# Attention outputs made feature-major, and projection panels moved between attention units and into the delta rule's scan

## What is computed

```python
# layer 0 of block one; H=8 heads of 64, causal (one block of 256 keys)
a_out = moba_attention(split_heads(q, MOBA_HEADS, MOBA_HEAD_DIM),
                       split_heads(k, MOBA_HEADS, MOBA_HEAD_DIM),
                       split_heads(v, MOBA_HEADS, MOBA_HEAD_DIM))
b_out = multiscale_pool(p, pool_w[i], pool_scale[i])
mix = jnp.concatenate([a_out, b_out], axis=-1) @ ev_w_out[i]
# both layers of block one; 4 heads of 256, keys and values from mem_n
q = (xn @ wq).reshape(B, S, XATTN_HEADS, XATTN_HEAD_DIM)
k, v = jnp.split(mem_n @ wkv, 2, axis=-1)
p = jax.nn.softmax(s, axis=-1).astype(v.dtype)
o = jnp.einsum('bhsm,bmhd->bshd', p, v).reshape(B, S, D)
return o @ wo
# layer 1 of block one: scan over 4 chunks of 64 tokens, per head
def step(state, inp):
    v_new = u_n - jnp.einsum('bhck,bhkv->bhcv', w_n, state)
    o = (jnp.einsum('bhck,bhkv->bhcv', qd_n, state)
         + jnp.einsum('bhij,bhjv->bhiv', qk_n, v_new))
    state = state * gl_n[..., None, None] + jnp.einsum('bhck,bhcv->bhkv', kd_n, v_new)
    return state, o
# both layers of block two: four attentions of 4 heads of 64; the first is
p = p[:, 0] - lam * p[:, 1]
o = sweep_query_blocks(block, q)
o = rmsnorm_2(o, norm_g) * (1.0 - lam_init)
y = jnp.concatenate([o_a, o_b, o_c, o_d], axis=-1) @ w_out[l]
```

## Time and profile before

| | us |
|---|---|
| runs | 2847.32, 2847.70, 2850.68 |
| median | 2847.7 |
| profiled execution | 2859.73 |
| its span, first to last instruction | 2857.9 |
| PE busy | 2739.3 (96%) |
| DVE busy | 1721.6 (60%) |
| ACT busy | 1309.5 (46%) |

### The profile page before, as it was taken

One profiled execution on the slowest core, in us unless ns is written; L12 is line 12 of the kernel. 1 busy time (PEld: TensorE's weight loads), 2 busy tenths in 40 slices (PEclk: granted clock), 3 DMA queues, 4 the chain that ended last, 5 costly groups with the idle time before them and its releaser, 6 DMA issues.

```text
span 2857.9 us, 39543 instructions
## 1 busy us (share of the span) xinstructions
PE 2739.3 (96%) x13974; PEld 2286.0 (80%) x13974; DVE 1721.6 (60%) x2575; ACT 1309.5 (46%) x1909; POOL 27.1 (1%) x40
## 2 busy tenths in 40 slices
PE   8999999997999999998999999899999999999998
PEld 7686898885778988885998886687878878787876
...
PEclk9899999896999999999999999899999999999999
...
GB/s 315 68 158 109 200 176 175 95 96 21 155 110 184 183 178 178 144 151 159 195 176 171 130 134 104 185 378 329 377 323 346 359 321 381 329 372 320 358 352 284
DMA packets 87635, 627.38 MB, mean 220 GB/s; under 512 B 9760, under 2 KB 9920, under 8 KB 12672
## 3 DMA queue, kind: packets, MB, share of 16 engines
...
...
## 4 chain that ended last, share of the span: by engine, by line
PE 94%; DVE 3%; ACT 1%; issue 1%; DMA 0%; DVEq 0%; SPq 0%; ACTq 0%
PE bank L775 21%; PE bank L668 14%; PE bank L523 11%; PE bank L803 11%; PE bank L682 6%; PE bank L618 6%; PE bank L534 6%; PE bank L864 6%; PE bank L590 2%; PE bank L566 2%; PE bank L913 1%; PE bank L818 1%; PE bank L745 1%; PE bank L579 1%; PE bank L790 1%
## 5 line engine op out<-in xcount | busy, mean ns | idle before, releaser
L1257 ACT ACTIVATE sb_parts<-sb_ring 128x1024 fp32r<-128x1024 f32 x873 | 873.0, 1052 | 95.6 <-PE bank L682 47.3
L1866 DVE TENSOR_TENSOR sb_parts<-sb_ring,sb_parts 128x1024 fp32r<-128x1024 f32 x675 | 787.0, 1219 | 6.3 <-ACT sb_parts L1257 6.3
L775 PE MATMUL bank<-sb_parts 128*128 128x512 f32 x2688 | 662.0, 396 | 8.2 <-DVE sb_parts L1866 5.7
L775 PEld LDWEIGHTS bank<-sb_parts 128*128 128x128 f32 x2688 | 495.6, 188 | 118.0 <-issue 9.5
L668 PE MATMUL bank<-sb_parts 128*128 128x256 f32 x3168 | 391.5, 286 | 20.1 <-DVE sb_parts L1830 20.1
L668 PEld LDWEIGHTS bank<-sb_parts 128*128 128x128 f32 x3168 | 390.3, 195 | 22.9 <-issue 20.8
L803 PE MATMUL bank<-sb_parts 128*128 128x512 f32 x1344 | 323.8, 390 | 0.0
L803 PEld LDWEIGHTS bank<-sb_parts 128*128 128x128 f32 x1344 | 251.7, 188 | 52.1
L1257 ACT ACTIVATE sb_REG<-bank 128x512 f32<-128x512 f32 (+3 forms) x118 | 67.8, 575 | 444.5 <-PE bank L523 224.3
L523 PE MATMUL bank<-sb_XT,sb_ring 128*128 128x256 f32 x1152 | 259.5, 387 | 6.9 <-DVE sb_XT L1698 3.9
L523 PEld LDWEIGHTS bank<-sb_XT,sb_ring 128*128 128x128 f32 x1152 | 222.7, 194 | 41.3 <-issue 10.4
...
## 6 DMA issues: line engine op xcount, KB each, us to landing
...
```

The costliest lines, as they stand in the source:

```text
L775: m = nc.tensor.matmul(banks[par][:, :], x[:, k, :], w[:, cols], start=k == 0 and t == 0, stop=k == KD - 1 and t == 2, skip_group_check=True)
L1257: return nc.scalar.activation(out, in_, ACT.Copy)
L1866: V_.tensor_tensor(LOW[u], ring[slot][:, 1024 * c:1024 * c + 1024], HIGH[u], ALU.subtract) \
```

## The change

Five things. (1) The mixing swaps its operands: V is stationary (64 or 128 columns), the transposed probabilities move (128 columns), and the output is feature-major. It is copied by ACT straight to `OT`, one bank for a group of units. `turn_outputs` is gone from the five attentions. (2) Since tokens now lie along the columns, the probabilities are scaled by the reciprocal row sums before their transposes: DVE in step s scales unit s-1 in SBUF (two operations of 128x256), and PE's transposes wait for that. (3) In s0 and s1 the norm of the first attention is done inside the units: 8 products of one column at step 13 sum the squares, 4 products of 128 columns at step 17 spread the factors. (4) Panels move into the units: both p panels and two key panels of x0 into MoBA, the four value panels into x0 and x1. SP loads two panels of `xattn_wkv` ahead of `ev_w_out` accordingly. (5) The last two key panels of x1 go into the scan, `su` moves ahead of `so`, and the state alternates between two halves of its tile.

The diff, cut to its core:

```diff
-        EARLY_KEYS = 2
+        EARLY_KEYS = 4
+
+
+        BESIDE = {"moba": {0: ("p", 0), 1: ("p", 1), 3: ("xk", 0, 2), 5: ("xk", 0, 3)},
+                  "x0": {j: ("xv", 0, j) for j in range(4)},
+                  "x1": {j: ("xv", 1, j) for j in range(4)}}
+        KEYS_FIRST = {0: (0, 1), 1: ()}
...
                             ada((key, s), 1, 6)
+                        if s in BESIDE.get(key, {}):
+                            name = BESIDE[key][s]
+                            if name[0] == "xv":
+                                panel_tok(name, lhs=MT, bank=6 + s % 2)
+                            elif name[0] == "xk":
+                                normed("mem")
+                                panel_T(name, rhs=MT, bank=6 + name[2] % 2)
+                            else:
...
-                        pe.wait_ge(sem("probs_ready"), base_unit[key] + t + 1)
+                        pe.wait_ge(sem("probs_scaled"), base_unit[key] + t + 1)
...
+                        name = ("mixed", key, u["group"])
                         wait_read(("turned", key, t))
-                        ps = claim(("mixed", key, t), 4 + t % 2)
-                        for j in range(2):
+                        if key[0] == "x" and u["tb"] == 0:
+                            wait_read(*[("xv", int(key[1]), 2 * (t // NT) + j) for j in range(2)])
+                        ps = claim(name, 4 + u["group"] % 2) if name not in turns else bank_in_turn(name)
+                        for j, c, rows, at in u["mix"]:
                             for kb in range(NT):
                                 o = (2 * j + kb) * P
-                                m = nc.tensor.matmul(ps[:, j * u["hd"]:(j + 1) * u["hd"]],
-                                                     PT[:, (base_unit[key] + t) % 2, o:o + P], u["v"][j][kb],
-                                                     start=kb == 0, stop=kb == NT - 1)
-                        filled(m, ("mixed", key, t))
+                                m = nc.tensor.matmul(ps[rows, at:at + P], u["v"][j][kb][c],
+                                                     PT[:, (base_unit[key] + t) % 2, o:o + P],
+                                                     start=kb == 0 and (u["turns"] == 1 or u["turn"] + u["tb"] + j == 0),
+                                                     stop=kb == NT - 1 and u["turn"] == u["turns"] - 1,
+                                                     skip_group_check=True)
+                        if u["last"]:
+                            filled(m, name)
+                        else:
+                            m.then_inc(sem("unit_mixed"), 1)
+                    if key[0] == "s" and s == DIFF_SUMS:
+                        pe.wait_ge(sem("diff_squares"), int(key[1]) + 1)
+                        ps = claim(("diff_sums", key), 6)
+                        for tb in range(NT):
+                            for h in range(HS):
+                                m = nc.tensor.matmul(ps[:, 4 * tb + h:4 * tb + h + 1], DSQ[:, h // 2, tb * P:tb * P + P],
+                                                     cst(f"half{h % 2}")[:, 0:1], start=True, stop=True)
+                        filled(m, ("diff_sums", key))
+                    if key[0] == "s" and s == DIFF_SPREAD:
+                        pe.wait_ge(sem("diff_inverse"), int(key[1]) + 1)
+                        ps = claim(("diff_spread", key), 7)
+                        for c in range(2):
+                            for tb in range(NT):
+                                m = nc.tensor.matmul(ps[:, c * T + tb * P:c * T + tb * P + P],
+                                                     DINV[:, tb, 2 * c:2 * c + 2, :].rearrange("p h n -> p (h n)"), ident,
+                                                     start=True, stop=True)
+                        filled(m, ("diff_spread", key))
+
+            def bank_in_turn(name):
+                return banks[turns[name][0]]
...
                 for j in range(4):
                     panel_T(("xq", layer, j))
-                for j in range(EARLY_KEYS if layer else 0, 4):
+                for j in KEYS_FIRST[layer]:
                     panel_T(("xk", layer, j), rhs=MT)
-                for j in range(4):
-                    panel_tok(("xv", layer, j), lhs=MT)
-                wait_read(*[(x, layer, j) for x in ("xq", "xk", "xv") for j in range(4)])
+                wait_read(*[(x, layer, j) for x in ("xq", "xk") for j in range(4)])
                 attention(f"x{layer}")
-                us = UNITS[f"x{layer}"]
-                wait_read(*[("mixed", f"x{layer}", t) for t in range(len(us))])
-                turn_outputs(n, list(range(8)))
+                wait_read(*groups_of(f"x{layer}"))
                 project(n)
...
                 products("wt", M_of(gKBE), M_of(gXT), tb)
+            panel_T(("xk", 1, 2), rhs=MT, bank=4)
...
-                ps = claim(("so", n))
-                for h in range(4):
-                    if n:
-                        nc.tensor.matmul(ps[rows, h * P:h * P + P],
-                                         flat(gQDT)[:, h * T + tb * P + base:h * T + tb * P + base + C64],
-                                         gST[:, h, :], start=True, stop=False)
-                    m = nc.tensor.matmul(ps[rows, h * P:h * P + P], gQK[rows, 4 * tb + h, rows], gVN[rows, h, :],
-                                         start=n == 0, stop=True)
-                filled(m, ("so", n))
...
+                if n == 1:
+                    panel_T(("xk", 1, 3), rhs=MT, bank=5)
+                ps = claim(("so", n))
+                for h in range(4):
+                    if n:
+                        nc.tensor.matmul(ps[rows, h * P:h * P + P],
+                                         flat(gQDT)[:, h * T + tb * P + base:h * T + tb * P + base + C64],
+                                         gST[:, 4 * (n % 2) + h, :], start=True, stop=False)
+                    m = nc.tensor.matmul(ps[rows, h * P:h * P + P], gQK[rows, 4 * tb + h, rows], gVN[rows, h, :],
+                                         start=n == 0, stop=True)
+                filled(m, ("so", n))
             pe.wait_ge(sem("delta_out"), 1)
...
+                    if s >= MIX_LAG + 1 and us[s - MIX_LAG - 1]["last"]:
+                        keep(key, us[s - MIX_LAG - 1])
...
+            def keep(key, u):
+
+                name = ("mixed", key, u["group"])
+                n = u["chunks"].stop - u["chunks"].start
+                cols = slice(0, T) if n == 2 else slice(u["tb"] * P, u["tb"] * P + P)
+                wait_full(act, name)
+                dst = OT[:, u["chunks"], cols]
+                m = copy(dst, bank_of(name)[:, :].rearrange("p (c t) -> p c t", c=n))
+                read_out(m, name)
+                if u["turns"] == 2:
+                    wait_drained(act, name)
+                    nc.scalar.activation(DSQ, dst, ACT.Square).then_inc(sem("diff_squares"), 1)
...
-                    if s >= MIX_LAG:
-                        t = s - MIX_LAG
-                        u = us[t]
+                    if s >= 1:
+                        t = s - 1
                         g = base_unit[key] + t
-                        name = ("mixed", key, t)
-                        wait_full(dve, name)
                         dve.wait_ge(sem("probs_ready"), g + 1)
                         ri = sm("row_inverse", 8)[:, 2 * (g % 4):2 * (g % 4) + 2]
                         step(V_.reciprocal(ri, RS[:, 2 * (g % 4):2 * (g % 4) + 2]))
-                        hd = u["hd"]
-                        ps = bank_of(name)
-                        if u["diff"]:
-
+                        if us[t]["turn"]:
                             step(V_.tensor_scalar(ri, ri, sm("neg_lambda", 1), None, ALU.mult))
-                            for j in range(2):
-                                m = V_.scalar_tensor_tensor(u["dst"][j], ps[:, j * hd:j * hd + hd], ri[:, j:j + 1],
-                                                            u["dst"][j], ALU.mult, ALU.add)
-                        else:
-                            for j in range(2):
-                                m = V_.tensor_scalar(u["dst"][j], ps[:, j * hd:j * hd + hd], ri[:, j:j + 1], None, ALU.mult)
-                        read_out(m, name)
+                        for j in range(2):
+                            m = V_.tensor_scalar(PR[:, g % 3, j, :], PR[:, g % 3, j, :], ri[:, j:j + 1], None, ALU.mult)
+                        m.then_inc(sem("probs_scaled"), 1)
+                    if s in BESIDE.get(key, {}):
+                        name = BESIDE[key][s]
+                        if name[-1] % 2:
+                            evac(name, beside(name))
+                    if key[0] == "s" and s == DIFF_SUMS:
+                        wait_full(dve, ("diff_sums", key))
+                        read_out(V_.tensor_scalar(sm("dms", 8), bank_of(("diff_sums", key))[:, 0:8], 1.0 / 64, EPS,
+                                                  ALU.mult, ALU.add), ("diff_sums", key))
```

(23 more changed lines are left out.)

147 lines of the change are left out of this document (78 added, 69 removed).

## The result

The changed kernel takes 2817.1 us, the median of four runs (2811.5 to 2819.5), beside 2847.5 us for the kernel before on the same chip: ratio 0.9887, 95% interval 0.9865 to 0.9909 (the two medians alone give 0.9893). So it is faster beyond the noise, by a little over 1%. The profiled execution took 2816.96 us (span 2815.1, mean granted clock 0.984); the one of before 2859.7 (span 2857.9, clock 0.967). So the time lies in the range of the prediction (2797 to 2827), 7 us above its likeliest value, and inside its own case (2803 to 2818). The share of PE's busy time is 96% in both; what differs is how much it does, and at which clock.

A forecast was written before the change was run, and what follows sets the result against it. It took PE, busy 96% of the span, as the bound, partly at half clock. Savings of 30.7+7.2 = 37.9 us turned the profiled 2859.7 into 2822, and the median 2847.7 into 2810; range 2797 to 2827.

The forecast's parts named there:

- its own case: Whole kernel: the prediction's main case, 2803 to 2818 us, chance 0.52.
- outside the kernel's steps: Whole kernel: the profile's 12 us above the median lie outside the steps, so 2822 profiled becomes 2810.
- a fall in the tail: MoBA: the clock falls again for the last 3.5 us of work, cost 3.5 with the projection's start; bounds 0 to 9.
- The 3.9 of real gain a layer: x0: of 17.8 us saved, 13.9 is two panels moved to MoBA, 3.9 real; x1 17.9, with 13.9 moved to the scan.
- sign of being wrong: Units and scan: transposes waiting for DVE over 0.3 us on average, or an `sw` still waiting for the state.
- the 4: Scan: the clock falls again for the last 4 us of work, cost 4; bounds 0 to 9.
- between -0.05 and +0.05 a unit: Mixing in 48 units with heads of 64: swapping operands is worth nothing by itself, at most 2.5 us either way.
- the cure of its slow panels: s1: denser mixing may cure three panels between units partly at half clock; between 0 and -5 us, taken as 0.
- A: Rival, whole kernel: the clock holds everywhere, about 50 us saved, 2798 us; chance 0.22.
- B: Rival: clock falls right behind the last panel in MoBA and scan, and behind one-column products; 24 saved, 2824; chance 0.2.
- C: Rival, slower: 64-column stationary counts as half the array, so s0 and s1 units get half clock; up to 190 us; chance 0.03.
- D: Rival: panels do nothing for the clock; short pieces in MoBA and scan run at half clock; 3 saved, 2844; chance 0.03.

The follow-up runs named there:

- e10: The kernel before, unchanged, profiled a second time: 2850.8 us.
- e2: The kernel before with only the panels moved into the units of MoBA and both cross attentions; token-major mixing, output transposes and old scan kept: 2838.9 us.
- e1: The changed kernel with all twelve panels taken out of the units of MoBA, x0 and x1; new mixing and new scan stay: 2825.1 us.
- e7: The changed kernel with the scan's new order but no panels in it; the two key panels stand ahead of x1: 2821.4 us.
- e5: The changed kernel with the key panel of scan step 1 moved behind the last `so` products: 2807.8 us.
- e4: The changed kernel with 128 instead of 64 columns of V as stationary tile in the mixing of the 48 units with heads of 64: 2812.5 us.

## Why the prediction was right, and where its steps failed

**In sum.** My terms made 37.9 us out of the profiled 2859.7. Measured against that same profile, the stretches I had priced give these gains (a minus is a loss): MoBA -2.8, x0 +17.3, scan +0.3, x1 +17.5, s0 -2.2, s1 +4.6, s1's projection +2.2: 36.9. Stretches that I had left alone gave another 6 (2.1 before MoBA, where the two profiles of the changed kernel differ by 1.9 as well, and 4.0 in the feed-forward stage behind s0), so the changed profile came out at 2817 and not at 2822.

**From profile to median: the step that failed.** I took the 12 us between the profile of before and its median for something "outside the kernel's steps" and carried it over: 2822 to 2810. The changed kernel has no such distance (profile 2817.0, median 2817.1). The distance lay inside the steps: e10's profile, 8.9 us faster than the first, has MoBA at 54.6 instead of 65.6, and 11.1 us is more than the whole difference. The change takes just that away; I counted it as gained and subtracted it again. (The clock in MoBA is known only for profiled executions, so that the median runs lacked the fall is likely, not shown.) Part of it was also a low median of three runs: against the median of 42 runs of before, 2851.0, the change gives 33.8, not 38, and against the four on its own chip 30.4.

**MoBA.** I had 52.5 at full clock and 3.5 for a fall in the tail, 56.0 in all from V's end; measured 54.5, without a fall (predicted and seen: clock 1.00 from 62 to 105 us). 2 us were missing from the full-clock sum: 8 units times 0.18 for the new mixing, and panels of 7.0 to 7.1 instead of 6.95 between units. The mechanism was half right. The clock held up to the last panel in nine profiles of nine, but the old order keeps it too in one of three (e10), so most of what I priced as cured was a draw of the profile. That the clock held in the tail is likewise no proof against the 3.5: in e2 it fell there.

**x0 and x1.** Predicted 17.8 and 17.9, measured 17.3 and 17.5. The 3.9 of real gain a layer, at 3.4 and 3.6, is 2.9 from the transposes and some 0.5 to 0.8 from filled waits (e2; 1.1 and 1.4 by e1). No transposes stand behind any of the five attentions and the projections start 1.09 to 1.25 us after the last product, as foreseen to 0.2. Neither sign of being wrong came: the transposes in the units wait for DVE once in MoBA (0.72 us), once in s0 (0.53) and once in s1 (0.75), far below 0.3 on average, and no `sw` waits for the state.

**Scan.** Predicted 38.5 plus 4 for the clock, 42.5; measured 41.4. Two errors that cancel. The clock held to the end of the work, so the 4 was 0; that is luck in part, as in e1 the same scan fell behind its second panel and took 45.3, 3.9 more. The full-clock sum was 2.9 short: `so` 2.89 instead of 2.5 a step 1.3 (I had halved the half-clock time; its pairs, which alternate between 128- and 64-row tiles, take 0.62 us at half clock and 0.36 at full, less than a halving, and no run shows why), a wait of 0.87 ahead of the first panel, panels 0.3, small pieces 0.4. My step "5.4 at full clock" was 5.9. What pays for the panels is the clock, when it holds (e7), more than the waits.

**s0 and s1.** Predicted 2.5 us shorter each; measured 2.2 longer and 4.6 shorter against the first profile, 1.2 longer and 3.0 shorter against the mean of three. The pieces I had were right: one-column products 1.95 (2.1), spreading 1.16 (0.9), tail stall 0.53 (0.7), clock behind the eight 1.3 in s0 (1.0) and none in s1. That 1.3 is a draw too: it is in both profiles of the changed kernel, and not in e1 or e5, which have the same eight. Missing is the term that I had declared worth "between -0.05 and +0.05 a unit": 0.18, over 20 units 3.6 us in each layer (e4 takes 3.4 and 3.0 of it back). With it s0 comes to 1.1 longer, close to the 1.2 against the mean of three. In s1 I had set the cure of its slow panels at 0 out of 0 to 5; the changed kernel has no slow one, and s1 ends 5.7 us below that 1.1 against the first profile, 3.4 against the other two. The nearest row that I had used for the new mixing, the scan's products of 128 columns, had a 128-wide stationary tile. Tiles of 64 columns stand in the trace before only in the scan, and where one follows a tile of 128 columns PE waits first (0.78 and 1.32 us), so no row there gave the price of the change; my bounds were drawn as if it could cost nothing.

**The rivals.** A (the clock holds everywhere, 2798) was right about MoBA and the scan of this kernel, but its time rested on the same carried-over 12 us and lacked the 0.18 a unit, 8.6 us in all. B didn't happen in MoBA and the scan of this kernel, though e1's scan and e2's MoBA show such a fall behind the last panel; behind the one-column products it took 1.3 us once. C and D fell: units with 64-column tiles ran at full clock, their scores 1.06 us. D's starting point was wrong in its own way: it took the half clock of the old order for certain.

**What stays open.** Why the dips of shared stretches come in some kernels and not in others isn't settled; the runs show only that they repeated in the two profiles of the changed kernel and vary, in MoBA above all, between the three of the kernel before. Some 10 of the 34 us lie there: the projections behind s0 and s1, the stages between, s1's slow panels. I can't say which edit brought them.
